# Merging two products of a triangular inverse in an RWKV-7 scan

## The chip, the cores and the metric

The kernel runs on all 8 cores of one Trainium2 chip. Each core takes one of the 8 prompts (2048 tokens) and 16 of the 128 samples (8 tokens each), with weights of its own copy and no exchange between cores. The metric is the device time of the slowest core in microseconds.

## The reference

One layer of a decoder reads x and runs three branches on the normalised input: a short convolution, RWKV-7, and attention to 256 memory tokens. Their gated outputs are summed, projected and added to x. The change touches RWKV-7 alone, whose state S (one 64 x 64 matrix for each of 16 heads) goes through the tokens in turn:

```
def _wkv_step(S, inp):
    r, w, k, v, kk, a = inp
    sa = jnp.einsum('bhvk,bhk->bhv', S, kk)
    S = (S * w[:, :, None, :] - sa[..., None] * (kk * a)[:, :, None, :]
         + v[..., None] * k[:, :, None, :])
    o = jnp.einsum('bhvk,bhk->bhv', S, r)
    return S, o
```

The kernel does 128 tokens at a time. Within such a chunk the terms `sa` depend on each other through a strictly triangular 128 x 128 matrix X, and the kernel needs the inverse Z = (I - X)^-1. Since X^128 = 0, this is the finite product (I + X)(I + X^2)(I + X^4) ... (I + X^64). For the samples the matrix falls into blocks of 8 tokens, and the product ends with X^4.

## The kernel before, in words

The tokens of a core go through in two passes: pass 0 has 1024 prompt tokens and the 128 sample tokens, pass 1 the other 1024 prompt tokens. In each pass the RWKV phase comes first, then convolution, attention and the output projection. The RWKV phase loops over 8 pairs of heads (`j`), and for each over blocks of 256 prompt tokens (4 in either pass), in pass 0 also one block of the 128 sample tokens. That makes 64 prompt blocks and 8 sample blocks.

A block goes through `prep` (projection matmuls, token shift, decay, key normalisation, on all engines), `scan_block` and `post` (group norm and gate). Blocks alternate between two sets of four PSUM banks and two sets of working tiles (`par` 0 and 1), so that two blocks can be under way together.

`scan_block` has up to four units, one for each chunk of 128 tokens and each head. A unit has one PSUM bank `ps[B + u]`. First the products of keys and receptance are masked into `uSB` and `uSK` (stage S2). `uXY` holds X and its transpose Y side by side in bfloat16, `uZ` the inverse so far, which starts as I + X. Then come NL levels (6 for prompts, 2 for samples), each in four loops over the units: two matmuls of 128 columns for the next X and Y, one copy of both from PSUM on ScalarE (256 columns), one matmul of 128 columns for the product of the new X with Z, and one addition of it to Z on VectorE. Behind the levels (S4, S5) Z is multiplied with keys and values, and the chunks follow each other through the state `M0b`.

In the trace the tiles of this stage carry the names of the buffers in which they lie: X and Y of `par` 0 are in `s_qTs`, those of `par` 1 and every Z in `s_U`, `uSB` in `s_memnT`, `uSK` in `s_KTb`. So an ACT CAST to `s_qTs` or `s_U` of 128x256 is one level of one unit of `par` 0 or 1, and a DVE TENSOR_TENSOR `s_U<-ps,s_U` is one addition to Z. The additions number 6 for each of the 256 prompt units and 2 for each of the 16 sample units, 1568 in all.

The order in which each engine gets its instructions is fixed at build time. `Prog.add` records every operation with the names it reads and writes. Reading a PSUM bank counts as writing it (`w = list(w) + psr`), so all work on one bank is in series, whichever columns it touches. `Prog.schedule` then plays the program with modelled costs and places, on each engine, the ready operation with the earliest start and, among those, the longest path behind it, looking 800 operations ahead. It also models the ScalarE function tables (`TSW`). On the chip each engine runs its list in that order, with semaphores between engines.

Of the kernel before, what the change touches and what calls it, by code (L numbers as in the profile page):

```python
# [289 lines left out]
def TT(out, in0, in1, op):  # L290
    return _tag(lambda e: e.tensor_tensor(out=out, in0=in0, in1=in1, op=op), out)  # L291
# [117 lines left out]
def build_nc(stages=("rwkv", "conv", "mem")):  # L409
# [12 lines left out]
    with ExitStack() as es:  # L422
# [524 lines left out]
        uXY = [dalloc(256).rearrange("p (a t) -> p a t", a=2) for _ in range(NU)]  # L947
        uZ = [dalloc(128) for _ in range(NU)]; uLV = [dalloc(64) for _ in range(NU)]
# [6 lines left out]
        def scan_block(j, nch, sample, ot, ko, par):  # L955
# [32 lines left out]
            for u, (c, hh) in enumerate(units):  # L988
                P.dve(TT(uXY[UB + u][:, 1, :], ps[B + u][:, 0:128], mLT, ALU.mult), r=[psk[B + u], "consts"], w=[f"uXY{UB + u}"])
                P.act(CPA(uLV[UB + u][:, :], ps[B + u][:, 384:448]), r=[psk[B + u]], w=[f"uLV{UB + u}"])  # L990
                P.pool(CP(uXY[UB + u][:, 0, :], uSB[UB + u][:, 0:128]), r=[f"uSB{UB + u}"], w=[f"uXY{UB + u}"])
                P.pool(TT(uZ[UB + u][:, :], uSB[UB + u][:, 0:128], identb[:], ALU.add), r=[f"uSB{UB + u}", "identb"], w=[f"uZ{UB + u}"])
            P.marks.append((f"S3_{j}", len(P.ops)))
            for n_ in range(1, NL + 1):
                for u in range(len(units)):
                    P.pe(MM(ps[B + u][:, 0:128], uXY[UB + u][:, 1, :], uXY[UB + u][:, 0, :], True, True), r=[f"uXY{UB + u}"], w=[psk[B + u]])
                    P.pe(MM(ps[B + u][:, 128:256], uXY[UB + u][:, 0, :], uXY[UB + u][:, 1, :], True, True), r=[f"uXY{UB + u}"], w=[psk[B + u]])
                for u in range(len(units)):
                    P.act(CPA(uXY[UB + u][:].rearrange("p a t -> p (a t)"), ps[B + u][:, 0:256]), r=[psk[B + u]], w=[f"uXY{UB + u}"])
                for u in range(len(units)):  # L1000
                    P.pe(MM(ps[B + u][:, 256:384], uXY[UB + u][:, 1, :], uZ[UB + u][:, :], True, True), r=[f"uXY{UB + u}", f"uZ{UB + u}"], w=[psk[B + u]])
                for u in range(len(units)):
                    P.dve(TT(uZ[UB + u][:, :], ps[B + u][:, 256:384], uZ[UB + u][:, :], ALU.add), r=[psk[B + u], f"uZ{UB + u}"], w=[f"uZ{UB + u}"])
# [207 lines left out]
```

How the kernel before makes its waits and increments, by code:

```python
    def emit(self, es):  # L191
# [39 lines left out]
            for key, val in wl.items():  # L231
                if wd.get(key, 0) >= val:
                    continue
                wd[key] = val
                sem = streams[key[1]] if key[0] == "d" else sems[key[1]]
                pend.append((sem, val))
            attach = None
            if pend and not op.dma and not os.environ.get("KNOATTACH"):
                attach = pend.pop()
            for sem, val in pend:
                eng.wait_ge(sem, val)
            ins = op.fn(eng)
            if attach is not None:
                ins._wait_ge(attach[0], attach[1])
            self.n_wait = getattr(self, "n_wait", 0) + len(pend)
            self.n_att = getattr(self, "n_att", 0) + (1 if attach else 0)
            if op.dma:
                scnt[op.stream] += 1
                op.sig_idx = scnt[op.stream]
                ins.then_inc(streams[op.stream], 16)
            elif op.signal:
                cnt[op.eng] += 1
                op.sig_idx = cnt[op.eng]
                ins.then_inc(sems[op.eng], 1)
            else:
                op.sig_idx = cnt[op.eng] + 1
        return len(ops)
```

## Time and profile before

| | |
|---|---|
| median of 2 runs | 3134.57 us (3130.4 to 3138.74) |
| the profiled execution | 3136.55 us, span of its slowest core 3135.2 us |
| the eight cores | 3104.4 to 3135.2 us, mean granted TensorE clock 0.777 to 0.792 |
| RWKV phase, pass 0 and 1 | about 143 to 1200 us and 1815 to 2740 us |
| busy share | PE 81%, DVE 61%, ACT 53%, POOL 36% |

The profile is that of the slowest core, 7. Work outside the span is 1.35 us (3136.55 less 3135.2). Busy shares are means over very different stages; PE counts as busy while a result drains, so a busy PE may still wait for other engines between its matmuls. Durations of short instructions on PE, DVE and ACT contain a latency that the next instruction on the engine overlaps: the distance from start to start is less than the duration.

### The profile page before, as it was taken

To read this page: it belongs to the slowest core of one execution; us is meant where nothing else is said; L and a number is where in the kernel's file an instruction comes from. 1 tells how busy PE (TensorE), PEld (TensorE's weight loads), DVE (VectorE), ACT (ScalarE), POOL (GpSimd) and SP (SyncE) were. 2 spreads that over 40 slices of the span, in tenths; PEclk is the share of its full clock that TensorE was granted. 3 is DMA by queue.
4 is the path that set the end of the run, shared out by engine and by line. 5 is a ranking of instruction groups with operands and counts; after the bars stand their busy time and mean duration, and the time that the engine had idled before them with its cause. 6 is when DMAs were issued, how large, how long until landed. Compare 5 with 4: busy or idle time off the path is not lost.

```text
span 3135.2 us, 52274 instructions; the slowest of 8 cores (3104.4 to 3135.2 us)
## 1 busy us (share of the span) xinstructions
PE 2552.0 (81%) x17531; PEld 1443.7 (46%) x17531; DVE 1916.7 (61%) x5317; ACT 1672.7 (53%) x4245; POOL 1119.3 (36%) x2151
## 2 busy tenths in 40 slices
PE   3688878888887889999859377878877878899998
PEld 2445444544544455554445144544544445444443
DVE  2577787777778774552303378777778777635244
ACT  3566666766666572123623366676766676621242
POOL 0244454434445431134334034344343343302333
PEclk9677676766767678999859677776866676799999
DMA  7300010000001002344493700000000000134424
GB/s 177 61 15 15 15 28 15 15 15 15 15 14 28 15 15 50 64 87 68 72 167 74 187 7 9 15 14 1 15 14 1 15 15 1 28 65 74 94 55 121
DMA packets 66962, 138.39 MB, mean 44 GB/s; under 512 B 38153, under 2 KB 38338, under 8 KB 57222
## 3 DMA queue, kind: packets, MB, share of 16 engines
q0 software_dynamic: 20016, 94.64, 17.8%
q1 hardware_dynamic: 46678, 40.42, 4.4%
q8 instruction: 138, 2.26, 0.3%
q14 instruction: 130, 1.06, 0.1%
HBM read 213.85 MB, written 15.82 MB: 73 GB/s over the span
## 4 chain that ended last, share of the span: by engine, by line
PE 63%; DVE 14%; ACT 11%; DMA 6%; issue 3%; POOL 2%; SPq 0%; DVEq 0%; ACTq 0%; POOLq 0%
PE ps L261 61%; ACT L281 5%; DVE s_tmp L294 4%; ACT s_tmp L281 4%; DVE s_tmp L291 3%; DMA s_xt<-xall 3%; PE ps L264 2%; DMA s_tmp<-cv 2%; DVE s_KTb L291 1%; DVE s_memnT L291 1%; DVE s_tmp L302 1%; DVE s_acc L294 1%; DMA s_xt<-mem 1%; ACT s_acc L308 1%; DVE s_tmp L288 1%
## 5 line engine op out<-in xcount | busy, mean ns | idle before, releaser
L261 PE MATMUL ps<-s_xnT,s_ring 128*128 128x512 bf16 (+2 forms) x5256 | 1027.9, 335 | 40.5 <-ACT s_tmp L308 18.4
L261 PEld LDWEIGHTS ps<-s_xnT,s_ring 128*128 128x128 bf16 x5256 | 503.6, 105 | 410.0 <-issue 21.9
L291 DVE TENSOR_TENSOR s_U<-ps,s_U 128x128 bf16<-128x128 f32 x1568 | 413.4, 287 | 96.8 <-PE ps L261 86.1
L281 ACT ACT_TABLE_LOAD x292 | 374.6, 1283 | 53.2 <-DVE s_tmp L291 31.2
L281 ACT ACTIVATE s_tmp<-ps 128x512 f32<-128x512 f32 (+4 forms) x384 | 175.1, 470 | 382.4 <-PE ps L261 349.6
L308 ACT CAST s_qTs<-ps 128x256 bf16<-128x256 f32 (+1 forms) x808 | 296.4, 439 | 91.0 <-PE ps L261 89.3
L261 PE MATMUL ps<-s_U 128*128 128x128 bf16 x2304 | 306.7, 243 | 32.6 <-ACT s_U L308 32.0
L308 ACT CAST s_U<-ps 128x256 bf16<-128x256 f32 x768 | 283.2, 456 | 25.9 <-PE ps L261 24.3
L291 DVE TENSOR_TENSOR s_tmp<-s_tmp 128x256 f32<-128x256 f32 (+3 forms) x504 | 215.5, 432 | 133.2 <-ACT s_tmp L281 96.8
L261 PE MATMUL ps<-s_qTs 128*128 128x128 bf16 x1600 | 268.6, 280 | 6.3 <-DVE s_U L291 2.5
L291 DVE TENSOR_TENSOR s_tmp<-ps,s_tmp 128x512 f32<-128x512 f32 (+2 forms) x168 | 97.1, 588 | 279.8 <-PE ps L261 267.1
L261 PE MATMUL ps<-s_acc 64*128 64x256 bf16 (+2 forms) x1072 | 234.7, 322 | 37.0 <-DVE s_KTb L291 33.6
L261 PE MATMUL ps<-s_yT,s_ring 128*128 128x512 bf16 (+1 forms) x960 | 233.4, 349 | 1.6 <-POOL s_yT L291 1.0
L287 POOL TENSOR_SCALAR s_Mst<-s_Mtmp,s_pc 128x64 f32<-128x64 f32 x128 | 70.9, 554 | 443.9 <-DVE s_Mtmp L291 443.9
L264 PE MATMUL ps<-s_identb,s_acc 128*128 128x128 bf16 x544 | 97.7, 299 | 161.1 <-DVE s_acc L294 104.5
L261 PEld LDWEIGHTS ps<-s_U 128*128 128x128 bf16 x2304 | 183.6, 109 | 79.7 <-ACT s_U L308 37.6
L261 PE MATMUL ps<-s_U,s_qTs 128*128 128x128 bf16 x800 | 206.2, 275 | 6.5 <-ACT s_qTs L308 5.8
L291 POOL TENSOR_TENSOR s_yT<-s_tmp 128x256 bf16<-128x256 f32 (+2 forms) x144 | 141.2, 982 | 134.3 <-ACT s_tmp L281 72.5
L291 POOL TENSOR_TENSOR s_acc<-s_tmp 128x256 bf16<-128x256 f32 (+1 forms) x216 | 164.1, 775 | 20.8 <-DVE s_tmp L294 12.1
L281 ACT ACTIVATE s_tmp<-s_tmp 128x256 f32<-128x256 f32 (+1 forms) x432 | 159.7, 401 | 19.1 <-DVE s_tmp L294 9.3
L261 PEld LDWEIGHTS ps<-s_qTs 128*128 128x128 bf16 x1600 | 144.5, 121 | 49.8 <-DVE s_U L291 16.1
L291 POOL TENSOR_TENSOR s_U<-s_memnT,s_identb 128x128 bf16<-128x128 bf16 x272 | 119.1, 451 | 120.6 <-DVE s_memnT L291 118.3
(190 smaller groups left out, 4397.1 us busy)
## 6 DMA issues: line engine op xcount, KB each, us to landing
s_ring<-wall POOLq DMA_DIRECT2D x74, 1024.0 KB, 8.8
s_xt<-xall SPq DMA_DIRECT2D x34, 512.0 KB, 4.9
y<-s_tmp SPq DMA_DIRECT2D x34, 256.0 KB, 3.9
s_acc<-swkv SPq DMA_DIRECT2D x16, 256.0 KB, 3.6
wkvs<-s_acc SPq DMA_DIRECT2D x16, 256.0 KB, 3.4
s_Kb<-ck POOLq DMA_DIRECT2D x16, 256.0 KB, 10.2
s_Vb<-cv POOLq DMA_DIRECT2D x16, 256.0 KB, 9.4
s_tmp<-ck POOLq DMA_DIRECT2D x16, 256.0 KB, 9.4
```

The lines of the kernel that those rows point to most:

```text
L261: return _tag(lambda e: e.matmul(out, lhsT, rhs, start=start, stop=stop), out)
L264: return _tag(lambda e: e.transpose(out, in_, ident), out)
L281: fn = _tag(lambda e: e.activation(out=out, in_=in_, func=func, **kw), out)
L287: return _tag(lambda e: e.tensor_scalar(out=out, in0=in0, scalar1=s1, scalar2=None, op0=op0), out)
L288: return _tag(lambda e: e.tensor_scalar(out=out, in0=in0, scalar1=s1, scalar2=s2, op0=op0, op1=op1), out)
L291: return _tag(lambda e: e.tensor_tensor(out=out, in0=in0, in1=in1, op=op), out)
L294: fn = _tag(lambda e: e.scalar_tensor_tensor(out=out, in0=in0, scalar=scalar, in1=in1, op0=op0, op1=op1), out)
L302: return _tag(lambda e: e.reciprocal(out=out, in_=in_), out)
L308: return _tag(lambda e: e.copy(out=out, in_=in_), out)
```

## The change

X, Y and Z of a unit are laid side by side in one buffer of 384 columns, as [Z | X | Y]. Z starts as the identity matrix instead of I + X. At each level one matmul with Y as weights and [Z | X] as the moving operand (256 columns) gives both the product of X with Z and the next X, and a second one (128 columns) the next Y. VectorE adds the first 128 columns to Z, and ScalarE copies the other 256. Because Z is now one level behind, a last product and addition follow the levels. For each prompt unit the matmuls go from 18 to 13, the additions from 6 to 7, the copies remain 6; for each sample unit 6 to 5, 2 to 3 and 2. On GpSimd the addition of the identity becomes a copy of it, which doesn't read `uSB`. The buffers are laid out anew in the same donors.

```
-        uXY = [dalloc(256).rearrange("p (a t) -> p a t", a=2) for _ in range(NU)]
-        uZ = [dalloc(128) for _ in range(NU)]; uLV = [dalloc(64) for _ in range(NU)]
+        uW = [dalloc(384) for _ in range(NU)]
+        uXY = [w_[:, 128:384].rearrange("p (a t) -> p a t", a=2) for w_ in uW]
+        uZ = [w_[:, 0:128] for w_ in uW]; uLV = [dalloc(64) for _ in range(NU)]
...
-                P.pool(TT(uZ[UB + u][:, :], uSB[UB + u][:, 0:128], identb[:], ALU.add), r=[f"uSB{UB + u}", "identb"], w=[f"uZ{UB + u}"])
+                P.pool(CP(uZ[UB + u][:, :], identb[:]), r=["identb"], w=[f"uZ{UB + u}"])
...
             for n_ in range(1, NL + 1):
-                for u in range(len(units)):
-                    P.pe(MM(ps[B + u][:, 0:128], uXY[UB + u][:, 1, :], uXY[UB + u][:, 0, :], True, True), r=[f"uXY{UB + u}"], w=[psk[B + u]])
-                    P.pe(MM(ps[B + u][:, 128:256], uXY[UB + u][:, 0, :], uXY[UB + u][:, 1, :], True, True), r=[f"uXY{UB + u}"], w=[psk[B + u]])
-                for u in range(len(units)):
-                    P.act(CPA(uXY[UB + u][:].rearrange("p a t -> p (a t)"), ps[B + u][:, 0:256]), r=[psk[B + u]], w=[f"uXY{UB + u}"])
-                for u in range(len(units)):
-                    P.pe(MM(ps[B + u][:, 256:384], uXY[UB + u][:, 1, :], uZ[UB + u][:, :], True, True), r=[f"uXY{UB + u}", f"uZ{UB + u}"], w=[psk[B + u]])
-                for u in range(len(units)):
-                    P.dve(TT(uZ[UB + u][:, :], ps[B + u][:, 256:384], uZ[UB + u][:, :], ALU.add), r=[psk[B + u], f"uZ{UB + u}"], w=[f"uZ{UB + u}"])
+                for u in range(nU):
+                    W = uW[UB + u]
+                    P.pe(MM(ps[B + u][:, 0:256], W[:, 256:384], W[:, 0:256], True, True), r=[f"uXY{UB + u}", f"uZ{UB + u}"], w=[psk[B + u]])
+                    P.pe(MM(ps[B + u][:, 256:384], W[:, 128:256], W[:, 256:384], True, True), r=[f"uXY{UB + u}"], w=[psk[B + u]])
+                for u in range(nU):
+                    W = uW[UB + u]
+                    P.dve(TT(W[:, 0:128], ps[B + u][:, 0:128], W[:, 0:128], ALU.add), r=[psk[B + u], f"uZ{UB + u}"], w=[f"uZ{UB + u}"])
+                for u in range(nU):
+                    W = uW[UB + u]
+                    P.act(CPA(W[:, 128:384], ps[B + u][:, 128:384]), r=[psk[B + u]], w=[f"uXY{UB + u}"])
+            for u in range(nU):
+                W = uW[UB + u]
+                P.pe(MM(ps[B + u][:, 0:128], W[:, 256:384], W[:, 0:128], True, True), r=[f"uXY{UB + u}", f"uZ{UB + u}"], w=[psk[B + u]])
+            for u in range(nU):
+                W = uW[UB + u]
+                P.dve(TT(W[:, 0:128], ps[B + u][:, 0:128], W[:, 0:128], ALU.add), r=[psk[B + u], f"uZ{UB + u}"], w=[f"uZ{UB + u}"])
```

## Rows read from the trace of the kernel before

**Rows 1.** The page, parts 1 and 4: busy time, chain that ended last.
```profile
PE 2552.0 (81%) x17531; PEld 1443.7 (46%) x17531; DVE 1916.7 (61%) x5317; ACT 1672.7 (53%) x4245; POOL 1119.3 (36%) x2151
...
PE 63%; DVE 14%; ACT 11%; DMA 6%; issue 3%; POOL 2%; SPq 0%; DVEq 0%; ACTq 0%; POOLq 0%
```

**Rows 2.** Windows (length; busy PE, PEld, DVE, ACT, POOL; PEclk; DMA, GB/s).
```profile
500.00:700.00 200.00, 165.87 (x1216) 98.58 (x1215) 150.01 (x446) 123.01 (x331) 86.42 (x175) 0.68 0.08 17
2000.00:2200.00 200.00, 162.21 (x1149) 94.17 (x1149) 151.75 (x473) 134.54 (x363) 79.66 (x170) 0.67 0.04 6
2250.00:2251.00 1.00, 1.00 (x12) 1.00 (x11) 0.32 (x2) 1.00 (x5) 0.19 (x1) 0.50 0.00 0
2256.00:2257.00 1.00, 1.00 (x14) 0.60 (x12) 1.00 (x5) 1.00 (x6) 0.00 (x0) 1.00 0.00 0
2243.00:2263.00 20.00, 19.94 (x185) 13.49 (x183) 16.66 (x66) 16.11 (x57) 4.13 (x13) 0.74 0.00 1
2267.00:2287.00 20.00, 12.93 (x87) 7.76 (x85) 11.98 (x30) 16.55 (x33) 8.56 (x20) 0.84 0.00 0
```

**Rows 3.** Chain that ended last, 2200 to 2320 us, pass 1.
```profile
2228.12 1.28 ACT L281
...
2234.43 1.27 DVE s_tmp L294 x2
...
2243.45 17.38 PE ps L261 x159
2260.83 0.04 issue
```

**Rows 4.** ScalarE in order of time, 2200 to 2320 us.
```profile
2243.89 0.67 ACT L308 CAST s_qTs<-ps 128x256 bf16<-128x256 f32 x2
...
2247.33 0.69 ACT L308 CAST s_qTs<-ps 128x256 bf16<-128x256 f32 x2 [1.73 <-PE ps L261]
...
2253.90 0.75 ACT L308 CAST s_U<-ps 128x256 bf16<-128x256 f32 x2
2254.43 0.78 ACT L308 CAST s_qTs<-ps 128x256 bf16<-128x256 f32 x2
2254.95 0.80 ACT L308 CAST s_U<-ps 128x256 bf16<-128x256 f32 x2
...
2259.13 0.67 ACT L308 CAST s_U<-ps 128x256 bf16<-128x256 f32 x2
...
2261.61 0.82 ACT L308 CAST s_U<-ps 128x256 bf16<-128x256 f32 x2 [0.53 <-PE ps L261]
...
2300.66 0.67 ACT L308 CAST s_qTs<-ps 128x256 bf16<-128x256 f32 x2
```

**Rows 5.** TensorE in order of time, 2240 to 2267 us.
```profile
2244.35 0.61 PE L261 MATMUL ps<-s_qTs 128*128 128x128 bf16 x4
...
2253.49 0.50 PE L261 MATMUL ps<-s_U 128*128 128x128 bf16 x6
...
2265.01 0.72 PE L261 MATMUL ps<-s_xnT,s_ring 128*128 128x256 bf16 x5
```

**Rows 6.** VectorE in order of time, 2240 to 2267 us.
```profile
2248.56 0.48 DVE L291 TENSOR_TENSOR s_U<-ps,s_consts 128x128 bf16<-128x128 f32 x2
```

**Rows 7.** Tile s_U: count, duration ns min/median/max.
```profile
L261 PE MATMUL ps<-s_U x2304: 219/219/315, 145.5 to 2727.7; 128*128 128x128 bf16 x192
L291 DVE TENSOR_TENSOR s_U<-ps,s_U x1568: 274/291/294, 143.6 to 2728.0; 128x128 bf16<-128x128 f32 x196
L291 POOL TENSOR_TENSOR s_U<-s_memnT,s_identb x272: 413/424/693, 135.9 to 2711.6; 128x128 bf16<-128x128 bf16 x136
L299 POOL COPY s_U<-s_memnT x128: 289/293/294, 144.9 to 2713.8; 128x128 bf16<-128x128 bf16 x128
```

**Rows 8.** The page, part 5: costliest groups.
```profile
L281 ACT ACT_TABLE_LOAD x292 | 374.6, 1283 | 53.2 <-DVE s_tmp L291 31.2
L308 ACT CAST s_qTs<-ps 128x256 bf16<-128x256 f32 (+1 forms) x808 | 296.4, 439 | 91.0 <-PE ps L261 89.3
```

More of the change, by code:

```diff
@@ L991, in scan_block @@
                 P.pool(CP(uXY[UB + u][:, 0, :], uSB[UB + u][:, 0:128]), r=[f"uSB{UB + u}"], w=[f"uXY{UB + u}"])
-                P.pool(TT(uZ[UB + u][:, :], uSB[UB + u][:, 0:128], identb[:], ALU.add), r=[f"uSB{UB + u}", "identb"], w=[f"uZ{UB + u}"])
+                P.pool(CP(uZ[UB + u][:, :], identb[:]), r=["identb"], w=[f"uZ{UB + u}"])
             P.marks.append((f"S3_{j}", len(P.ops)))
+            nU = len(units)
             for n_ in range(1, NL + 1):
-                for u in range(len(units)):
-                    P.pe(MM(ps[B + u][:, 0:128], uXY[UB + u][:, 1, :], uXY[UB + u][:, 0, :], True, True), r=[f"uXY{UB + u}"], w=[psk[B + u]])
-                    P.pe(MM(ps[B + u][:, 128:256], uXY[UB + u][:, 0, :], uXY[UB + u][:, 1, :], True, True), r=[f"uXY{UB + u}"], w=[psk[B + u]])
```

## The prediction, made blind

> **What bounds the kernel now.** I began with the page. TensorE is busy 81% of the span and has 63% of the chain that ended last [rows 1], which makes it look like the bound. The windows by stage say otherwise [rows 2]: in the RWKV phase of either pass (lines 500 to 700 and 2000 to 2200 us) PE, DVE and ACT are busy 81 to 83%, 75 to 76% and 62 to 67%, and the granted TensorE clock is 0.67 to 0.68 on average, so TensorE keeps falling to its lower level of 1.2 GHz (0.50, line 2250 to 2251) and coming back to 2.4 GHz (1.00, line 2256 to 2257). No engine is full; work is handed round.
>
> Next I followed ScalarE in order of time through pass 1 [rows 4]. The pattern repeats: the first level copy of `par` 0 starts at 2243.89 us, and its counterpart at 2300.66, so a period is 56.8 us. It covers two blocks (48 level copies). There are 64 prompt blocks, so 32 such pairs; pass 0 has the same pairs with a sample block behind every second one. In a period the levels of both blocks overlap and stand in one stretch of 20 us, from 2243 to 2263 (in rows 2 PE 19.94, DVE 16.66, ACT 16.11 us busy). The other 37 us are projections, `prep`, masks and `post`: from 2267 to 2287 ScalarE is busiest with 16.55 of 20 us, and the chain runs through function table loads of 1.28 us and VectorE's preparation [rows 3]. The change doesn't touch those 37 us.
>
> Within the 20 us I see two regimes. From 2253.90 to 2254.95 four copies start in 1.05 us [rows 4], that is 0.264 us each, and their durations grow from copy to copy while none is preceded by idle time: ScalarE is full. Six matmuls of 128 columns take 0.50 us there [rows 5]; less the 0.219 of the last [rows 7], five starts take 0.28, or 0.056 us each. Three per unit and level are 0.17 us, well under 0.264. VectorE's addition occupies 0.20 us (two in 0.48 with the first at 0.28) [rows 6], also under it. Outside this stretch a level waits for its own chain. `par` 0 goes from level 1 to level 2 in 2247.33 - 2243.89 = 3.44 us, with ScalarE idle 1.73 us for TensorE, and the last level of `par` 1 comes 2261.61 - 2259.13 = 2.48 us after the one before [rows 4]; both blocks in full step would take 8 x 0.264 = 2.11.
>
> **What the change adds and removes.** I make the sum against the profiled execution, 3136.55 us, and subtract 2 us at the end for the median (3134.57).
>
> 1. *Copies.* Number and size stay: 48 x 0.264 = 12.7 us per pair. Where ScalarE is full, nothing is gained. The change in that part: 0.
>
> 2. *One visit to TensorE fewer per level.* At 2.4 GHz a level before is the second of two matmuls (0.056 + 0.219), the copy (0.37, its length alone, as two take 0.67 with the second 0.26 to 0.30 behind), the product (0.219), the addition (0.28), and four handovers of 0.04 [rows 3 to 7]: 1.30 us. After, the first matmul takes twice 0.056, then 0.219 + 0.28 + 0.37 + 3 x 0.04 = 1.10. At 1.2 GHz four matmuls take 0.61, and with 0.29 for the last they are 0.107 apart [rows 5]; a level goes from 0.107 + 0.29 + 0.37 + 0.29 + 0.28 + 0.16 = 1.50 to 0.213 + 0.29 + 0.28 + 0.37 + 0.12 = 1.27. I take 0.2 us for each level that waits for its chain. By the copies these are levels 1 and 2 of `par` 0 and 5 and 6 of `par` 1: 4 x 0.2 x 32 = -26 us. Bounds: 0 (another wait ends last) to -26.
>
> 3. *Queueing.* The two of these levels that the rows show take 3.44 and 2.48 us against 1.3 to 1.5 of pure chain, 2.0 and 1.1 us more. As an estimate for the mean of the four I take 1.2 us of standing behind other instructions, in four visits, 0.3 each. One visit fewer could give 4 x 0.3 x 32 = -38 us; but the other block's masks and chunk steps that are queued there stay, so I take a quarter, -10. Bounds 0 to -38, and beyond this the second rival.
>
> 4. *The last product and addition.* 0.219 + 0.28 + 2 x 0.04 = 0.58 us at the end of the levels. For `par` 1 it lies on the path to S4 and S5, since nothing but its own chain is left: 32 x 0.58 = +19. For `par` 0 ScalarE's full stretch hides it; were that cover gone, +37 for both.
>
> 5. *TensorE's columns.* Per prompt unit 18 x 128 = 2304 before, 6 x 384 + 128 = 2432 after. The extra 128 columns in 272 units cost 272 x 0.107 = 29 us at 1.2 GHz, 272 x 0.056 = 15 at 2.4. They fall at the end of the levels, where the clock is high and a part is counted in 4; I take +4, bounds 0 and +29.
>
> 6. *VectorE.* 272 more additions of 0.20 us are 54 us. Those of `par` 0 go into the 0.06 us per unit and level that VectorE has left where ScalarE is full; of `par` 1 the last is in 4 and the others run beside the products. I take 0; with that cover gone +35 (54 less the 19 of term 4).
>
> 7. *New waits.* The copy now waits for the addition on the same bank, where it waited for TensorE. Behind it in ScalarE's queue stand the copies of other units, and behind those the tables and activations of `prep`; who waits is the next level. VectorE was in the same loop before (the next products waited for its addition), so the visit is moved and not new: 0, inside the bounds of 3. The first matmul of a block now waits for Z too. GpSimd's copies of X take 0.29 us and the additions 0.42 [rows 7]; a copy of the identity, priced like the former, saves 272 x 0.13 = 35 us of GpSimd, which is the idlest engine, and may be done early as it reads nothing of the block. If it is queued ahead of the copies of X it costs up to 0.29 per block, 64 x 0.29 = +19; if the shorter list lets X come sooner, the same as a gain. I take 0.
>
> 8. *Sample blocks.* Two levels and a last round in place of two: 8 x (0.58 - 0.4) = +1.
>
> Sum: -26 - 10 + 19 + 4 + 1 = -12, so 3124 for the profiled execution and 3122 for the median. With the bounds of the path terms, -26 - 38 and nothing lost gives 3070, and no gain with 37 + 29 gives 3201.
>
> TensorE's matmuls at 2.4 GHz follow each other at 0.056 us for 128 columns [rows 5], each with its own weights, so loads are hidden and fewer loads are worth nothing. The Trainium skill, "TensorE: Matmul & The Clock Gate", section Back-to-back issue gap, says that in a stream of load and matmul pairs both ops set the spacing, about 81 ns at 128 columns and 131 at 512. By that figure, called an estimate, 18 matmuls would be 1.46 us per unit and 13 at most 7 x 0.081 + 6 x 0.131 = 1.35, so the change would relieve TensorE by at least 0.1 us. The trace does not agree.
>
> **The rivals.**
>
> *ScalarE is the whole story.* The 12.7 us of copies and the 37 us outside are what count, and the shortened levels only wait for them; the last round is hidden as well. For it: ScalarE's full stretch. Against: 20 - 12.7 = 7.3 us per pair in which it isn't full. Gives 3135.
>
> *The stalls between the blocks go.* The matmuls of a level are one group and no longer two, so an instruction of the other block at the head of TensorE's list stops it once per level. If half of the 7.3 us comes back, less 0.6 for the last round, that is 3 us per pair, 96 us: 3135 - 96 = 3039. For it: the idle 1.73 us before level 2 [rows 4]. Against: in this part the masks fill VectorE, and they stay.
>
> *The last round and the extra columns are paid in full* (the other side). Place: where `par` 0 ends while `par` 1 is in its levels, on VectorE, 8 additions of 0.20 us per pair, with TensorE's 128 columns per unit at 1.2 GHz. Price 54 + 29 = +83 us: 3218. It becomes slower than 2% (63 us) once three quarters of it are on the path and nothing of the hop is regained. For it: VectorE is at 16.66 of 20 us there and the clock is at 0.50 in the first half. Against: the rounds fall where the clock is high.
>
> *The order changes elsewhere.* All lists are worked out anew, with a level of another length. There are 292 table loads of 1.28 us [rows 8]. One more or fewer per pair is 32 x 1.28 = 41 us either way, 3094 or 3176; one more per block 3217. Nothing in the trace tells the sign.
>
> *A matmul has a price of its own, whatever its columns.* Then 1296 matmuls fewer (4704 to 3408) would give 1296 x 0.056 = 73 us of TensorE, and half of that where it is on the path: 3099. Against it: five matmuls of 256 columns take 0.72 us, 0.11 each [rows 5], twice those of 128. The skill's figure above would go the same way.
>
> **How the numbers follow.** Chances: forecast 0.46, ScalarE alone 0.15, stalls go 0.17, paid in full 0.08, order 0.12, price per matmul 0.02. The likeliest is 3122. The range has to reach into the stalls on one side and the order and the full price on the other: 3045 to 3190. A difference under 2% is about what a measurement of this kernel can't tell from none. Faster by more: 0.17, and 0.04 from the forecast's lower end, 0.02 from the order, together 0.23. Slower by more: 0.08, 0.02 from the upper end, 0.03 from the order, 0.13. Within: 0.64.
>
> **What would show it.** In the changed kernel the copies in the full stretch should again start 0.264 us apart; the distance from level 1 to level 2 of `par` 0 should shrink from 3.44 by 0.2 to 0.5; additions to Z should number 1568 + 272 = 1840; the stretch of levels should last 19 to 20 us, and the period about 56.5. I am wrong if the period changes by over 2 us while the stretch doesn't (then it is the order, and the table loads will differ from 292), if the stretch falls under 18 us (stalls), or if it grows beyond 21.

## The result, and the profile after

The changed kernel is 2% slower: the ratio of its time to that of the kernel before is 1.02, with a 95% interval of 1.016 to 1.024 (3199.5 to 3205.7 us against 3130.4 to 3139.8). Both programs have executions in which something outside them slows a group of four cores by some per cent; every ratio here leaves those out, so the plain median of the changed kernel, 3264.97 us, says little, and of e17, whose profiled execution is such a one, the table below has the mean of the four cores that were not slowed. The profiled execution took 3204.97 us, its slowest core 3203.8, its eight cores 3189.3 to 3203.8. I had forecast 3122 us, and the time lies outside my range of 3045 to 3190.

The page of the changed kernel, parts 1, 4 and 5, against [rows 1, 8]:

```profile
PE 2609.9 (81%) x16235; PEld 1393.1 (43%) x16235; DVE 1971.7 (62%) x5589; ACT 1714.9 (54%) x4265; POOL 1068.5 (33%) x2151
...
PE 60%; DVE 16%; ACT 12%; DMA 6%; issue 3%; POOL 2%; SPq 0%; ACTq 0%; DVEq 0%; POOLq 0%
...
L281 ACT ACT_TABLE_LOAD x312 | 400.3, 1283 | 51.8 <-DVE s_tmp L291 27.6
```

TensorE has 1296 matmuls fewer and is busy 58 us longer, VectorE has 272 instructions more, and there are 20 more table loads. Windows of the changed kernel, to be laid beside [rows 2]: the granted clock in the RWKV phase is 0.66 and 0.69, where it was 0.68 and 0.67; the third line is a stretch of levels, the last the time behind it.

```profile
500.00:700.00 200.00, 164.27 (x1073) 92.76 (x1073) 145.17 (x437) 121.31 (x313) 76.32 (x165) 0.66 0.05 12
2000.00:2200.00 200.00, 163.77 (x995) 84.96 (x995) 154.51 (x502) 135.16 (x363) 71.66 (x164) 0.69 0.06 12
2243.00:2263.00 20.00, 19.29 (x135) 10.55 (x133) 18.18 (x72) 15.55 (x55) 4.73 (x13) 0.73 0.01 2
2267.00:2287.00 20.00, 20.00 (x106) 10.97 (x106) 10.29 (x29) 11.61 (x26) 9.45 (x23) 0.57 0.11 18
```

The level stretch looks as I expected, with more of VectorE (18.18 for 16.66 us). The 20 us behind it, which I had called untouched, don't look so: the granted clock is 0.57 where [rows 2] have 0.84, and TensorE is busy 20.00 us for 12.93. (This pair stands 2 us later, and the one of [rows 2] is of the better kind; how many are of which follows.)

ScalarE in order of time in the changed kernel, answering to [rows 4]. The buffers have moved; per level `par` 0 has two copies to `s_qTs` and two to `s_U`, `par` 1 three to `s_U` and one to `s_xt`.

```profile
2245.78 1.08 ACT L308 COPY s_xnb<-ps 128x512 bf16<-128x512 bf16 x2
2246.73 0.69 ACT L308 CAST s_qTs<-ps 128x256 bf16<-128x256 f32 x2
...
2249.64 0.37 ACT L308 CAST s_qTs<-ps 128x256 bf16<-128x256 f32 x1 [1.16 <-DVE s_qTs L291]
...
2255.33 1.25 ACT L308 CAST s_U<-ps 128x256 bf16<-128x256 f32 x4
...
2257.44 1.36 ACT L308 CAST s_U<-ps 128x256 bf16<-128x256 f32 x4
```

Where ScalarE is full, from 2255.33 to 2257.44, eight copies take 2.11 us, 0.264 each as before. Level 1 to level 2 of `par` 0 takes 2249.64 - 2246.73 = 2.91 us, where it took 3.44 (2.91 or 2.92 in 15 pairs of pass 1 on the slowest core, and 3.44 in 14 of 15 before). And the copies now wait for VectorE's addition where they waited for TensorE.

**A ruler for the pairs.** VectorE's `s_Mtmp<-ps,s_Mst` occurs once per chunk and pair of heads (a chunk step), so four times in a pair of blocks, two for `par` 0 and two for `par` 1. Here are the first and the fourth of two pairs of the kernel before, and of one of the changed kernel in the second fence:

```profile
2261.40 0.23 DVE L291 TENSOR_TENSOR s_Mtmp<-ps,s_Mst 128x64 f32<-128x64 f32 x1 [0.23 <-PE ps L261]
2273.73 0.22 DVE L291 TENSOR_TENSOR s_Mtmp<-ps,s_Mst 128x64 f32<-128x64 f32 x1
2318.13 0.23 DVE L291 TENSOR_TENSOR s_Mtmp<-ps,s_Mst 128x64 f32<-128x64 f32 x1 [0.23 <-PE ps L261]
2333.77 0.22 DVE L291 TENSOR_TENSOR s_Mtmp<-ps,s_Mst 128x64 f32<-128x64 f32 x1 [1.07 <-PE ps L261]
```

```profile
2263.55 0.21 DVE L291 TENSOR_TENSOR s_Mtmp<-ps,s_Mst 128x64 f32<-128x64 f32 x1
2279.87 0.23 DVE L291 TENSOR_TENSOR s_Mtmp<-ps,s_Mst 128x64 f32<-128x64 f32 x1 [1.06 <-PE ps L261]
```

I call the time from first to fourth the *spread* and from there to the next pair's first the *gap*. Two neighbouring pairs of one program have spreads of 12.33 and 15.64 us. Windows over them show why, in the kernel before:

```profile
2264.00:2274.00 10.00, 9.86 (x75) 5.92 (x75) 5.97 (x19) 6.48 (x14) 2.70 (x7) 1.00 0.01 2
2317.00:2321.00 4.00, 3.91 (x41) 2.40 (x37) 2.59 (x12) 2.36 (x8) 0.45 (x1) 1.00 0.00 0
2321.00:2334.00 13.00, 13.00 (x66) 6.41 (x65) 5.92 (x19) 7.58 (x15) 2.70 (x7) 0.53 0.00 1
```

and in the changed one:

```profile
2263.00:2267.00 4.00, 3.91 (x31) 2.25 (x29) 2.97 (x12) 1.90 (x7) 0.97 (x3) 1.00 0.01 2
2267.00:2280.00 13.00, 13.00 (x66) 6.23 (x66) 5.83 (x18) 7.49 (x15) 3.74 (x11) 0.52 0.00 0
```

The clock comes up in the levels in every pair. Either it stays at 1.00 through the chunk steps, or it falls to 0.50 behind the first (2.5 to 3.6 us in the kernel before, 2.3 to 4.7 in the changed one, over the pairs of pass 1 on all cores) and the rest goes slower. Matmuls of 256 columns behind them show at which level of the clock they ran, in the kernel before and in the changed one:

```profile
2270.70 0.83 PE L261 MATMUL ps<-s_xnT,s_ring 128*128 128x256 bf16 x6
```

```profile
2276.70 1.46 PE L261 MATMUL ps<-s_xnT,s_ring 128*128 128x256 bf16 x6
```

Over all cores, 87 of 128 pairs of pass 1 keep the clock in the kernel before, with a mean spread of 12.2 us, and 41 lose it, with 15.6. In the changed kernel 36 keep it (12.5) and 92 lose it (16.4).

The table has the kernels on which the reading rests. Pass 0 and pass 1 are from the first chunk step to the last; A is spread plus gap of a pair of pass 0 with no sample block behind it, B with one; gap, spread and kept are of pass 1 (kept: pairs of 16 with a clock over 0.90 in the spread). All are means over the eight cores of the profiled execution (e17: four), in us.

| kernel | ratio | table loads | pass 0 | A | B | pass 1 | gap | spread | kept |
|---|---|---|---|---|---|---|---|---|---|
| before | 1 | 292 | 1021.6 | 50.3 | 85.6 | 871.9 | 43.9 | 13.3 | 10.9 |
| changed | 1.020 | 312 | 1072.7 | 51.5 | 90.5 | 893.6 | 43.3 | 15.3 | 4.5 |
| e1 | 1.017 | 292 | 1059.8 | 52.6 | 88.2 | 882.3 | 45.3 | 12.6 | 14.8 |
| e3 | 1.020 | 312 | 1077.8 | 52.7 | 90.0 | 882.2 | 43.5 | 14.4 | 7.0 |
| e4 | 1.040 | 312 | 1096.6 | 52.2 | 93.1 | 908.1 | 44.3 | 15.2 | 5.6 |
| e5 | 1.025 | 292 | 1062.8 | 52.0 | 89.3 | 910.1 | 44.9 | 14.8 | 5.6 |
| e6 | 1.032 | 292 | 1063.1 | 54.5 | 86.6 | 927.7 | 44.4 | 16.3 | 0 |
| e7 | 1.014 | 292 | 1034.6 | 51.3 | 86.1 | 886.6 | 43.9 | 14.3 | 11.2 |
| e8 | 1.027 | 310 | 1082.0 | 53.0 | 90.3 | 898.8 | 43.8 | 15.1 | 4.2 |
| e13 | 1.013 | 292 | 1053.5 | 52.4 | 87.5 | 885.1 | 44.6 | 13.5 | 11.6 |
| e15 | 1.019 | 292 | 1058.1 | 52.6 | 88.0 | 917.5 | 44.1 | 16.0 | 0 |
| e16 | 1.010 | 292 | 1052.3 | 53.0 | 86.7 | 881.3 | 45.1 | 12.8 | 13.8 |
| e17 | 0.993 | 292 | 1020.1 | 50.0 | 85.7 | 860.6 | 44.0 | 12.6 | 15.5 |
| e18 | 1.021 | 292 | 1067.0 | 54.4 | 87.2 | 891.5 | 44.4 | 14.1 | 9.8 |

**Where the time went.** Pass 0 has 51.1 us more, pass 1 21.7 us, together 72.8 (the mean span of the cores rose from 3121.3 to 3194.4). In pass 1 the gaps are 0.6 to 0.7 us *shorter*, 15 of them -10 us, and the spreads 2.0 us longer, +32. In pass 0 the eight A pairs make 8 x 1.3 = 10 us and the eight B pairs 8 x 4.9 = 39; the remaining 2 us come from the last B pair, which has no shortened gap behind it. In both kinds the gaps are 1.8 us shorter, while the spreads grow by 3.1 us in A and 6.7 in B. For the A pairs the granted clock doesn't explain that: their spreads are 16.8 us where it stays over 0.90 and 16.9 where it doesn't, against 13.4 and 14.9 before.

ScalarE in a B pair, between the chunk steps of `par` 0 and those of `par` 1, in the kernel before and then in the changed one:

```profile
489.17 1.28 ACT L281 ACT_TABLE_LOAD   x1
490.46 0.42 ACT L281 ACTIVATE s_tmp<-s_tmp 128x256 f32<-128x256 f32 x1
490.79 0.35 ACT L308 CAST s_U<-ps 128x256 bf16<-128x256 f32 x1
...
491.74 1.28 ACT L281 ACT_TABLE_LOAD   x1
```

```profile
505.88 1.28 ACT L281 ACT_TABLE_LOAD   x1
507.17 0.37 ACT L281 ACTIVATE s_tmp<-ps,s_hv 128x128 f32<-128x128 f32 x1
507.44 0.64 ACT L308 CAST s_U<-ps 128x256 bf16<-128x256 f32 x2
...
508.99 1.28 ACT L281 ACT_TABLE_LOAD   x1
510.28 0.93 ACT L281 ACTIVATE s_tmp<-s_tmp 128x256 f32<-128x256 f32 x3
511.11 0.90 ACT L308 CAST s_U<-ps 128x256 bf16<-128x256 f32 x3
...
512.30 1.28 ACT L281 ACT_TABLE_LOAD   x1
```

The sample block's `prep` brings loads and activations into `par` 1's levels. Before, a unit's copies stood between them singly, each unit at its own level. Now the four units go in step, and a level costs a load, its activations and four copies: 508.99 to 512.30 is 3.3 us. Besides, fewer of `par` 1's level copies are done when `par` 0 has made its second chunk step: 15 are left, where 11 were (counted in these two pairs).

### The profile page after: what moved, and what is told of

Read it like the earlier page. It is cut to its first block, busy times and chain, and to the rows that moved or that the text cites. A ratio compares the mean times of both kernels' runs of the same rounds, so it can differ in the third digit from the quotient of the medians.

```text
span 3203.8 us, 52229 instructions; the slowest of 8 cores (3189.3 to 3203.8 us)
## 1 busy us (share of the span) xinstructions
PE 2609.9 (81%) x16235; PEld 1393.1 (43%) x16235; DVE 1971.7 (62%) x5589; ACT 1714.9 (54%) x4265; POOL 1068.5 (33%) x2151
## 3 DMA queue, kind: packets, MB, share of 16 engines
q0 software_dynamic: 20016, 94.64, 16.9%
## 4 chain that ended last, share of the span: by engine, by line
PE 60%; DVE 16%; ACT 12%; DMA 6%; issue 3%; POOL 2%; SPq 0%; ACTq 0%; DVEq 0%; POOLq 0%
PE ps L261 58%; ACT L281 5%; DVE s_tmp L294 4%; ACT s_tmp L281 3%; DVE s_tmp L291 3%; DMA s_xt<-xall 3%; PE ps L264 2%; DMA s_tmp<-cv 2%; DVE s_KTb L291 1%; DVE s_memnT L291 1%; ACT s_U L308 1%; DVE s_acc L299 1%; POOL s_tmp L291 1%; DVE s_tmp L302 1%; DVE s_acc L294 1%
## 5 line engine op out<-in xcount | busy, mean ns | idle before, releaser
L261 PE MATMUL ps<-s_xnT,s_ring 128*128 128x512 bf16 (+2 forms) x5256 | 1047.6, 341 | 28.9 <-ACT s_xnT L311 9.3
L261 PE MATMUL ps<-s_U 128*128 128x128 bf16 (+1 forms) x2080 | 385.7, 287 | 55.3 <-ACT s_U L308 50.8
L308 ACT CAST s_U<-ps 128x256 bf16<-128x256 f32 x960 | 337.5, 447 | 70.5 <-DVE s_U L291 51.6
L291 DVE TENSOR_TENSOR s_U<-ps,s_U 128x128 bf16<-128x128 f32 x1120 | 299.6, 287 | 69.8 <-PE ps L261 59.7
L308 ACT CAST s_xt<-ps 128x64 bf16<-128x64 f32 (+1 forms) x464 | 144.9, 322 | 118.9 <-DVE s_qTs L291 78.5
L261 PE MATMUL ps<-s_qTs 128*128 128x128 bf16 (+1 forms) x912 | 182.1, 313 | 10.4 <-ACT s_qTs L308 3.9
L308 ACT CAST s_qTs<-ps 128x256 bf16<-128x256 f32 (+1 forms) x424 | 153.3, 422 | 45.3 <-DVE s_qTs L291 36.3
L281 ACT ACTIVATE s_tmp<-s_tmp 128x256 f32<-128x256 f32 (+1 forms) x432 | 157.9, 401 | 12.2 <-DVE s_tmp L294 4.1
L308 ACT COPY s_tmp<-ps 128x128 f32<-128x128 f32 (+1 forms) x176 | 57.2, 325 | 194.3 <-PE ps L261 186.0
L261 PE MATMUL ps<-s_tmp,s_blkb 128*128 128x256 bf16 (+1 forms) x288 | 97.5, 356 | 72.6 <-DVE s_tmp L291 60.5
L261 PEld LDWEIGHTS ps<-s_acc 64*128 64x128 bf16 (+1 forms) x1072 | 84.1, 118 | 161.2 <-DVE s_KTb L291 67.8
```

The source lines that it names most:

```text
L261: return _tag(lambda e: e.matmul(out, lhsT, rhs, start=start, stop=stop), out)
L281: fn = _tag(lambda e: e.activation(out=out, in_=in_, func=func, **kw), out)
L308: return _tag(lambda e: e.copy(out=out, in_=in_), out)
```

## The experiments

Eighteen kernels ran. In most of them the content of the levels and the order of the lists are taken apart: the planned order of one kernel is imposed on the other, operation by operation, so that order and levels can be told apart. "Old order" is that of the kernel before. All eighteen lay their buffers out as the changed kernel does, those with the old levels too; e11 (old levels, almost the old order) has a ratio of 1.0034, 292 table loads, 10.9 pairs kept and a pass 1 of 871.7 us for 871.9, so the layout costs little, if anything.

**e1: the new levels in the old order.**

```
-        order = self.schedule()
+        order = convert(order_of_kernel_before)   # addition n just ahead of copy n; the last product and addition where the old last ones stood
```

> The merged levels with their last round, but every engine gets its instructions in the order that was planned for the old levels; the two matmuls of a level stand where the old two stood, the addition just ahead of the copy, and the last product and addition where the old last ones stood. Theory A (the loss comes from the new plan, which lets the two blocks end together and puts more function table loads between the levels): ratio to before 0.99 to 1.00. Theory B (the loss lies in the new work itself, the seventh round and the copy that waits for the addition): 1.015 to 1.02, as the changed kernel.

1.0166 (1.0142 to 1.0191), 292 table loads. So some four fifths of the loss stay without any new plan, but in other places: the clock is kept in 14.8 of 16 pairs, more than before, and the gap is 1.4 us longer. The copies of the first level, in order of time on ScalarE:

```profile
2283.51 0.59 ACT L315 COPY s_xnb<-ps 128x512 bf16<-128x512 bf16 x1
2285.01 0.37 ACT L315 CAST s_qTs<-ps 128x256 bf16<-128x256 f32 x1 [0.91 <-DVE s_qTs L298]
2285.66 0.37 ACT L315 CAST s_qTs<-ps 128x256 bf16<-128x256 f32 x1 [0.27 <-DVE s_qTs L298]
```

They stand behind the addition, while VectorE is full of masks; before, none of them waited ([rows 4], 2243.89). From the first copy of the block's transposed inputs (`s_xt<-ps` 128x512, which the recorded expectations call the projection copy) to the first level copy pass 1 has 9.9 us, where it had 9.1 (such stage times are means over 15 pairs of the slowest core). In the changed kernel's own order it has 9.4.

**e2: the merged matmul split again**, 19 matmuls of 128 columns per unit in the order of the changed kernel.

```
-  MM(ps[B+u][:, 0:256], W[:, 256:384], W[:, 0:256])
+  MM(ps[B+u][:, 0:128], W[:, 256:384], W[:, 0:128]); MM(ps[B+u][:, 128:256], W[:, 256:384], W[:, 128:256])
```

> The changed kernel in its own order, with the matmul of 256 columns cut into two of 128, so 19 matmuls per prompt unit in place of 13. If merging itself neither helps nor harms (columns are what counts): 1.02 as the changed kernel, within 0.3%. If TensorE's clock falls more often because it has fewer matmuls to do: the clock comes back in pass 1 behind the levels and the ratio falls to 1.01. If a matmul has a price of its own: 1.03 or more.

1.0221 (1.02 to 1.0241), like the changed kernel: that the two products are one matmul neither gains nor costs.

**e3: the last round left out** in the order of the changed kernel.

```
-  for u: MM(ps[B+u][:, 0:128], W[:, 256:384], W[:, 0:128]); TT(W[:, 0:128], ps[B+u][:, 0:128], W[:, 0:128], add)
```

> The changed kernel in its own order without the last product and addition, so that the factor I + X^64 (for samples I + X^4) is left out of the inverse. Theory A: the last round is worth the 0.6 us per pair of blocks that I put on the path, 32 x 0.6 = 19 us, ratio 1.014. Theory B: it is worth most of the loss, ratio 1.00 to 1.005.

1.0195 (1.0175 to 1.0215), above what either theory had. Pass 1 is 11 us shorter than in the changed kernel (7.0 pairs kept for 4.5, the gap no shorter) and pass 0 5 us longer. In this order the last round isn't the cause.

**e4: a matmul more per level and unit**, result unused.

```
+  MM(ps[B+u][:, 384:512], W[:, 128:256], W[:, 256:384])
```

> The changed kernel in its own order with one more matmul of 128 columns per level and unit, whose result nobody reads, so that TensorE has at least as much to do as before. If the clock falls behind the levels of pass 1 because TensorE does less: the distance from the first to the last chunk step of a pair falls back from 16 to 12.3 us in most pairs and the ratio to 1.01 or less. If the clock's fall has another cause: 1.02 to 1.03.

1.0402 (1.0315 to 1.0489). The clock is kept in 5.6 pairs of 16 for 4.5, and each pair pays more. A matmul more in every level doesn't hold the clock.

**e5: the copy ahead of the addition**, new levels, old order: the copy waits for TensorE alone, the addition for the copy.

```
-  for u: TT(W[:, 0:128], ps[B+u][:, 0:128], ...)     then  for u: CPA(W[:, 128:384], ps[B+u][:, 128:384])
+  for u: CPA(W[:, 128:384], ps[B+u][:, 128:384])     then  for u: TT(W[:, 0:128], ps[B+u][:, 0:128], ...)
```

> The new levels in the planned order of the kernel before, as e1_new_levels_old_order (ratio 1.0166), but in every level ScalarE's copy stands ahead of VectorE's addition on the bank: the copy waits for TensorE alone, and the addition waits for the copy. Same instructions. Theory A (the copy's new wait for the addition is what costs in e1): the ratio falls from 1.0166 to 1.000-1.006, and in pass 1 the way from a pair's first level copy to its first chunk step goes from 18.2 us back to about 17.5, and the time between the projection copy and the first level copy from 9.9 back to about 9.1. Rival B (the cost is the last product and addition and VectorE's 272 more additions): the ratio stays at 1.014-1.019. Rival C (the addition is merely late now and the next level's product waits for it instead, the same visit): also 1.014-1.019, but the idle time moves from ScalarE's copies to TensorE's product.

1.0245 (1.0231 to 1.026), slower than e1. The 9.9 us went back to 9.1, as theory A had it, but the first level copy to the first chunk step went from 18.2 to 18.9: the addition is still in the loop, and the next product waits for it. The clock is kept in 5.6 pairs for 14.8. Theory A names a real wait and the wrong cure: the visit moved on to the product, as rival C said, though at a higher price than C gave it.

**e6: the last round left out, old order.** The edit is that of e3 in e1.

> The new levels in the planned order of the kernel before, without the last product and addition (the factor I + X^64, and I + X^4 for the samples, is left out of the inverse). Against e1_new_levels_old_order (1.0166) this prices the last round alone, with the order held. Theory A (the copy's wait costs): 1.010-1.016, so the last round is worth 0.2 us per pair or my 0.58 at most (-6 to -19 us, 1.0105 at the lower end). Rival B (the last round and its additions are what costs): 1.000-1.006, over 32 us less than e1.

1.0315 (1.0295 to 1.0335). With less work than e1 it is slower: no pair of pass 1 on any core keeps the clock, and it falls up to 2 us ahead of the first chunk step instead of some 3 behind it. The gap is 0.9 us shorter, which is what the last round costs where the clock is left out of it. Neither theory had this.

**e7: fillers in the chunk steps of the kernel before.**

```
+  MM(ps[B+3][:, 256:512], identb, loraW[:, 0:256]) x2   # per chunk step
```

> The kernel before in its own order, with two filler matmuls of 256 columns (identity times a weight tile, result unused) on TensorE in each chunk step of the prompt blocks, 512 more in all over 256 steps. Theory D (in pairs in which the granted clock falls to 0.50 behind the first chunk step the four steps take 15.6-16.2 us instead of 12.3, and the clock falls because TensorE has little to do there): the clock stays at 1.00 in all pairs of pass 1, their spreads are 12.5-13.2, and the time falls by 20-35 us (6 of 16 cold pairs in pass 1 and some in pass 0, 3.4 us each, less 0.2-0.4 us per pair for the fillers): ratio 0.989-0.994. Rival E (the clock falls for another reason, for instance a share of all cores' power, or the fillers stand in the chain): the cold pairs stay and the time grows by 32 x 4 x 0.1-0.2 us = 13-26 us, ratio 1.004-1.008.

1.0138 (1.0123 to 1.0153). The trace has 256 matmuls from `loraW` more, two in each of 128 chunk steps, and not the 512 that the expectation states. 11.2 pairs are kept for 10.9, the kept spreads are 13.0 us for 12.2 and the others 17.3 for 15.6: the fillers of four chunk steps cost 0.8 us at the high level of the clock and 1.7 at the low one, and the clock falls as before. That refutes theory D, and the price is above rival E's.

**e8: the copy ahead of the addition, in an order of its own.** The edit is that of e5, and the planner's order is used.

> The changed kernel with ScalarE's copy ahead of VectorE's addition in every level, in an order that the kernel's planner worked out anew for it. Theory F (the change's 68 us come in two parts: some 50 us by what the new levels cost in any order, and the rest by the order planned for them): if the copy's wait is the first part, this kernel comes to 1.000-1.010, with table loads anywhere from 292 to 312. Rival G (the planned order is the larger part, and any order planned for levels of this shape has both blocks in step and more cold pairs): 1.015-1.025, with 305 or more table loads and 10 or more of 16 pairs of pass 1 cold.

1.0266 (1.0252 to 1.0281), 310 loads, 4.2 of 16 pairs kept: rival G, a little above its range.

**e9 to e12: both kernels with another look-ahead.**

```
-    def schedule(self, window=800):
+    def schedule(self, window=500):    # e9, e10; 700 in e11, e12
```

> The kernel before with one number changed, the planner's look-ahead from 800 to 500 operations, so that the engines' lists differ in some hundred places and the instructions are the same. Theory L (the order of the lists and the clock that follows from it are a draw, whatever the levels): this moves the time by 0.5-2% either way, 0.98-1.02. Theory M (the order matters little, the new levels cost of themselves): 0.997-1.005.

> The changed kernel with the planner's look-ahead of 500 as in e9_old_lookahead_500. Theory L: 0.99-1.04, and divided by e9 a quotient that differs from 1.02 by over 0.008. Theory M: the quotient to e9 is 1.016-1.024 again, as in the two plans measured so far (1.02 in its own, 1.0166 in that of the kernel before).

> The kernel before with a look-ahead of 700, a smaller change of the lists (mostly TensorE's and GpSimd's). Theory L: 0.99-1.01, with the pairs of pass 1 that keep the clock at 1.00 anywhere from 4 to 16 of 16 (9 to 13 before). Theory M: 0.998-1.002 and 9 to 13 such pairs.

> The changed kernel with a look-ahead of 700. Theory L: its quotient to e11_old_lookahead_700 lies outside 1.012-1.028. Theory M: inside 1.016-1.024. In both, if the clock decides pass 1 as I read it, each pair more that keeps the clock at 1.00 is 3.3 us less from the first chunk step of pass 1 to the last, on every core.

Measured: 1.0055 (1.0031 to 1.0079), 1.0241 (1.0223 to 1.0259), 1.0034 (0.9995 to 1.0072), 1.0219 (1.0199 to 1.0239). The quotients of new to old levels are 1.0241 / 1.0055 = 1.0185 and 1.0219 / 1.0034 = 1.0184, each uncertain by some 0.003 to 0.004. That is theory M for the levels: the loss isn't a bad draw of one order. The old levels alone moved by slightly more than M allowed (1.005 and 1.002). Pairs kept are 10.6, 6.9, 10.9 and 3.8, table loads 297, 313, 292 and 310, so each new plan for the new levels brings 16 to 18 more loads, as the first brought 20.

**e13 and e14: the first level without its product**, in the old order and in its own. The change starts with Z = I and so multiplies X with the identity in level 1; here Z starts as I + X, by GpSimd's addition as in the kernel before.

```
+  level 1: MM(ps[B+u][:, 128:256], W[:, 256:384], W[:, 128:256]) only, no addition
```

> The new levels, but Z starts as I + X as in the kernel before, and the first level computes only X^2 and its transpose, two matmuls of 128 columns and a copy, with no product and no addition (the product of X with the identity was work of the change alone). Then five merged levels and the last round: 13 matmuls, 2304 columns and 6 additions per unit, columns and additions as in the kernel before. In the planned order of the kernel before. Theory N (what costs in e1_new_levels_old_order, 1.0166, is the first level's addition, behind which the copies of the first level stand while VectorE is full of masks): the time between projection copy and first level copy in pass 1 goes from 9.9 back to 9.1 us, the gap between pairs from 45.35 to 44.3-44.6, ratio 1.002-1.009 if the clock is kept as in e1. Rival P (the last round in the chain costs, wherever the additions stand): the gap stays at 45.1-45.4, ratio 1.014-1.018.

> The same program as e13_skip_first_old_order in the order that the planner works out for it. Against the changed kernel (1.02): theory N gives 1.003-1.012 (272 additions and 272 times 128 columns less), and in pass 1 a gap of 42.3-42.8 us where the changed kernel has 43.2. Rival Q (the loss is the plan for levels with ScalarE's copy last, table loads among the levels of the pairs with a sample block, and pairs without the full clock): 1.015-1.022, table loads 305 or more, spreads of 25 us and more in those pairs.

e13: 1.0125 (1.0109 to 1.014), gap 44.6 for e1's 45.3, pass 0 6 us shorter. Theory N has the mechanism and the size of the gap, not the ratio: the 11 us that the gaps gave in pass 1 were lost again, since the clock was kept in 11.6 pairs for 14.8. e14: 1.0117, but 0.9925 to 1.0309, so the ratio decides nothing. Its passes are 12 and 2 us shorter than the changed kernel's, its gap 43.3, 310 loads, 5.1 pairs kept: what N gives in the first term, and Q in the rest.

**e15: copy first and no last round, old order** (edits of e5 and e3 together).

> e5_copy_first_old_order (1.0245) without the last product and addition as well (the factor I + X^64, and I + X^4 for the samples, is left out). Account of the gap between pairs in pass 1: 43.9 before, +0.8 for the copy's wait, +0.95 by the last round (45.35 less 44.4). If these two are all, the gap is 43.7-44.1 here and 37 and 65.2 in pass 0; if the merging costs of itself, 44.4 or more. Of the time: with the clock lost in most pairs as in e5 and e6, 1.018-1.028; if it were kept, 0.998-1.004.

1.0189 (1.0058 to 1.032), no pair kept, gap 44.1. The account of the gap in pass 1 closes within 0.2 us of the 43.9 before; in pass 0 it doesn't (37.7 and 66.3 for 36.5 and 65.4).

**e16: the last round's matmul without its addition, old order.** Against e6, one matmul of 128 columns per unit is put back, whose result nobody reads.

> e6_no_last_round_old_order (1.0315, none of 16 pairs of pass 1 keeps the clock) with the last round's matmul put back and its addition still left out (the factor I + X^64 is computed and not added). Theory R (TensorE's own work at the end of the levels decides whether the clock holds through the chunk steps): 8 or more of 16 pairs keep it, ratio 1.010-1.020. Rival S (the delay by the addition decides, through when the chunk steps fall against the clock's rise): 0 to 3 pairs, ratio 1.028-1.034.

1.0096 (1.0071 to 1.0122), against e6's 1.0315. 13.8 of 16 pairs keep the clock, for none. Windows around the first chunk steps of a pair, e6 first, e16 second:

```profile
2330.00:2334.00 4.00, 3.17 (x28) 1.68 (x28) 2.19 (x9) 3.40 (x13) 0.00 (x0) 0.98 0.00 0
2334.00:2350.00 16.00, 15.93 (x82) 7.62 (x81) 7.24 (x23) 8.68 (x20) 3.19 (x8) 0.50 0.01 2
```

```profile
2296.00:2300.00 4.00, 3.64 (x35) 2.28 (x36) 2.37 (x10) 3.46 (x13) 0.00 (x0) 1.00 0.00 0
2300.00:2312.00 12.00, 11.94 (x96) 7.11 (x96) 7.09 (x23) 7.51 (x19) 3.02 (x7) 1.00 0.01 2
```

28 matmuls in the 4 us ahead of the chunk steps, and the clock falls with them; 35, and it holds. The number alone isn't the rule. In the kernel before, the pair that lost the clock at 2321 us had 43 in the 4 us ahead of its first chunk step:

```profile
2314.00:2318.00 4.00, 3.94 (x43) 2.62 (x44) 3.46 (x14) 3.39 (x13) 0.00 (x0) 1.00 0.02 6
```

The gap says what the round costs: 0.7 us by its matmul (45.1 less 44.4), 0.2 by its addition (45.3 less 45.1).

**e17 and e18: the same put to use in the kernel before**, one matmul more behind the products of each of levels 5 and 6, or (e18) one matmul of Y with Z behind the last addition.

```
   MM(ps[B+u][:, 256:384], uXY[u][:, 1, :], uZ[u])
+  MM(ps[B+u][:, 384:512], uXY[u][:, 1, :], uXY[u][:, 0, :])   # e17, levels 5 and 6
```

> The kernel before in its own order, with one matmul of 128 columns more per prompt unit behind the product of levels 5 and 6 (X with its transpose into a free part of the unit's bank, nobody reads it): 512 matmuls more, directly behind the product, so that the addition waits some 0.06 us longer. Theory R (TensorE's work at the end of the levels holds the clock through the chunk steps): 14 to 16 of 16 pairs of pass 1 keep it instead of 9 to 13, worth 3.3 us each, less 0.1-0.4 us a pair for the matmuls: the first chunk step to the last of pass 1 860-870 us instead of 867-878, ratio 0.993-0.999. Rival T (the phase of the work against the clock's steps decides, and more matmuls merely shift it): 0 to 12 pairs, ratio 1.001-1.02.

> The kernel before in its own order, with one matmul of 128 columns more per prompt unit, which stands behind the last addition to Z as the last round's does in the changed kernel, and whose result nobody reads: 256 matmuls more. Its cost in the chain was 0.7 us a pair in the new levels (gap 45.1 with it, 44.4 without): +22 us if the same here. Theory R: 14 to 16 of 16 pairs keep the clock, -10 to -16 us, in all 1.000-1.004. Rival T: 0 to 12 pairs, 1.005-1.02.

e17: 0.9927 (0.9895 to 0.9959), faster than both kernels, with 512 matmuls more. 15.5 of 16 pairs keep the clock, the gap is 44.0 for 43.9, and pass 1 is 11.3 us shorter. The 23 us of the ratio are of the slowest core; the mean of the cores falls by 17 us (3124.6 to 3107.7), and the rest is that the cores end closer together. Windows of one pair's chunk steps, on core 5:

```profile
2189.00:2193.00 4.00, 3.92 (x41) 2.41 (x38) 2.62 (x11) 2.04 (x7) 0.45 (x1) 1.00 0.02 6
2193.00:2203.00 10.00, 9.70 (x75) 5.80 (x73) 6.12 (x19) 6.63 (x14) 2.75 (x7) 1.00 0.00 0
```

e18: 1.021 (1.0125 to 1.0295), 9.8 pairs kept, and pass 0 45 us longer. Of the A pairs of pass 0, 6 of 64 over all cores keep the clock, where 49 did, and their spreads are 3.1 us longer, 24 of the 45 us. So theory R, that TensorE's work at the end of the levels holds the clock, comes true in e17 and fails in e18: behind the last addition, in the chain, the matmul does harm.

## Why the prediction was wrong

**Step 1 (copies)** held: 0.264 us per copy, and the full stretch as before.

**Steps 2 to 4 (one visit fewer, queueing, last round)** gave -26 - 10 + 19 = -17 us, with 5 and 8 -12. Where only these terms act, they came: in pass 1 the first level copy to the first chunk step went from 17.50 to 16.73 us and the gap from 43.9 to 43.3. That is -0.6 to -0.8 us per pair, -20 to -25 for 32, more than the sum. Level 1 to 2 of `par` 0 shrank by 0.53 us (0.2 to 0.5 forecast). The last round was priced too low. Its matmul and addition (step 4, 0.58 us a pair) and its columns (step 5, 4 us or 0.1 a pair) cost 0.9 of the gap in the old order, 0.7 of it the matmul's (e6, e16).

**Step 7 (the copy's wait for the addition, priced at 0) failed.** I reasoned that the visit to VectorE is moved and not new. But in level 1 it *is* new: the old first copies read TensorE's result with no addition ahead. With Z = I the first addition does no useful work and stands in VectorE's fullest stretch. In the old order this is 0.8 us per pair ahead of the first copy (e1, back in e5), and 0.7 of the gap (e13). In the changed kernel's own order it is 0.3 ahead of the first copy, and leaving out the first product and addition shortens the two passes by 14 us of the 73 (e14). I had written that the masks fill VectorE in this part, and had drawn nothing from it for this step.

**Step 8 (sample blocks, +1 us), and the sentence that the change doesn't touch what lies outside the levels, failed most.** The B pairs cost 39 us. The new plan puts `par` 1's levels in step and behind the table loads of the sample's `prep`; 20 loads more are 20 x 1.283 = 26 us of ScalarE. e1, without them, has 88.2 us for a B pair against 90.5, so by this comparison the plan makes 2.3 of the 4.9 us and the levels 2.6 (in the old order; no other order was compared so). I had this as the rival of the changed order, with 0.12, but as something for 32 pairs alike; its test (another number of loads than 292) came true.

**No step at all had the clock.** I read that it falls and comes back, and took it as given. It isn't: it was kept in 4.5 of 16 pairs for 10.9, and 6.4 pairs by 16.4 - 12.5 = 3.9 us are 25 us, more than pass 1's loss of 21.7. I also misread the period: 56.8 us runs through the chunk steps of a pair that keeps the clock (12.33 us), and not every pair does; the mean in pass 1 was 43.9 + 13.3 = 57.2, and it is now 58.6. The test that I had set, a period changed by over 2 us while the stretch stays, was too coarse for pass 1.

**The rivals.** ScalarE as the whole story and the stalls' end did not come. Nor did the last round in full (83 us): it is 0.9 us a pair, 29 us, in the old order (e6), and the time hardly moves without it in the new one (e3). The price per matmul is refuted by e2.

**What is shown and what isn't.** Shown: new levels cost 1.7 to 2% in the old order and under three plannings of their own; in the old order, taking out the last round's matmul loses the clock and putting it back regains it (e6, e16); matmuls behind levels 5 and 6 keep it in more pairs of the kernel before (e17). Not shown is what in TensorE's work decides it: 43 matmuls in 4 us ahead of the chunk steps lost it in one pair, 35 kept it in another, and e18 added work and gained nothing. Only argued: that in the changed kernel's own order the clock is lost for the same reason. e1 has the same instructions and keeps it, so there it is the order, and e4 tried a remedy that failed. The place of e17 wasn't tried in the changed kernel. Open as well: why the spreads of pass 0 grow in the changed kernel's own order even where the clock stays, where the other 21 us of e18's pass 0 went, and the 1.2 us that the gaps of the A pairs have too much in e15. The Z product in a bank of its own, which would free the copy of the addition and the addition of the copy, wasn't tried: all eight banks are taken. Nor was the copy at the same time as the addition on one bank.

## What to carry to other kernels

When a loop is merged, look at its first turn: a start value that makes the first product trivial has put a new operation, with its wait, into the busiest place. When TensorE goes back and forth between its two levels, count the repetitions that keep the high one before costing any edit: here one repetition is worth 3.4 to 3.9 us, some five times what the edit gained per pair, and an edit that removes TensorE's work can lose it. And impose the old order on the new program before blaming the plan or the content; it costs one run and splits the loss.

## What the hardware showed that I had not expected

Less work was slower and more was faster: leaving out the last round in e1 cost 1.5% (1.0166 to 1.0315), putting back its matmul alone gained 2.1% (to 1.0096), and 512 matmuls that nobody reads made the kernel before 0.7% faster. The same instructions in the same program had mean spreads of 12.2 us where the granted clock stayed and 15.6 where it fell. The Trainium skill, "TensorE: Matmul & The Clock Gate", section HAM oscillation — how this bites in real kernels, tells of a loop that falls back to the low level at each wait for DMA. The traces agree that a fall can come back loop after loop, but not that each repetition pays: 41 of 128 pairs did in one kernel and all of them in another (e6). And no transfer was waited for between the levels and the chunk steps; the clock fell behind stretches in which TensorE had 28 to 43 matmuls in 4 us.
